# Last quarters of the last two down matrices, read from a copy in eight groups of rows

## The reference, cut to what matters

```python
# hierarchical_moe, 32 experts, top 2 for each of the 256 tokens, for layer l = 0 and 1
hid = jax.nn.silu(xb @ w_gate[e]) * (xb @ w_up[e])      # w_gate, w_up: 1024 x 512 per expert
y = (hid @ w_down[e]) * g_b[:, None]                    # w_down: 512 x 1024 per expert
x = x + (sum of y over each token's experts)
# behind layer 0: a recurrent mixer (lru); behind layer 1: the second block (gated feed-forward, mixers)
```

## Time and profile before

| | us |
|---|---|
| median of the three runs shown | 2074.73 |
| lowest, highest | 2074.47, 2076.21 |
| span of the profiled execution, first to last instruction | 2072.5 |
| tail of layer 0: SP's first quarter to the end of the wait for the last | 500.6 to 532.1 |
| tail of layer 1, the same | 1019.4 to 1053.0 |

### The profile page before, as it was taken

How to read it: one execution, slowest core, us unless ns; L and a number is a source line. 1 busy time by engine, 2 the same in 40 slices (tenths; PEclk the granted TensorE clock), 3 DMA queues, 4 the chain that set the end, 5 groups by cost and what they waited for, 6 DMA issues and landing times.

```text
span 2072.5 us, 31532 instructions
## 1 busy us (share of the span) xinstructions
PE 1855.8 (90%) x13948; PEld 1441.8 (70%) x13948; DVE 1014.3 (49%) x1434; ACT 703.5 (34%) x1049; POOL 39.2 (2%) x46
## 2 busy tenths in 40 slices
PE   9987777677998876777799999999999999999999
PEld 7944333343795433343478889998888888999888
DVE  5722110111672110111158777877777667787666
ACT  6310000000561000000055555655546445465553
POOL 0000000000000000000000003000000000300000
PEclk9999998888999988899899999999999999999999
DMA  9899999999989999999985554545555556445552
GB/s 396 335 418 430 430 431 429 430 430 426 397 333 415 429 431 429 430 430 431 425 327 194 192 207 174 182 170 185 184 204 193 190 183 216 174 160 183 187 195 86
DMA packets 64942, 626.59 MB, mean 302 GB/s; under 512 B 7200, under 2 KB 7328, under 8 KB 14496
## 3 DMA queue, kind: packets, MB, share of 16 engines
q1 hardware_dynamic: 64800, 624.50, 75.4%
HBM read 623.42 MB, written 1.05 MB: 301 GB/s over the span
## 4 chain that ended last, share of the span: by engine, by line
PE 73%; DMA 19%; DVE 4%; ACT 2%; SPq 2%; issue 1%; DVEq 0%; ACTq 0%
PE ps L606 14%; PE ps L609 7%; PE ps L869 7%; DMA dense_ring<-in_moe_w_down 7%; PE ps L550 6%; PE ps L551 6%; PE ps L552 6%; DMA expert_ring_a<-in_moe_w_down 5%; PE ps L860 5%; PE ps L1093 4%; PE ps L1072 4%; DMA work<-in_moe_w_down 4%; PE ps L885 3%; PE ps L849 3%; PE ps L1077 2%; PE ps L1097 2%
## 5 line engine op out<-in xcount | busy, mean ns | idle before, releaser
L1674 DVE TENSOR_TENSOR w_lo<-dense_ring,w_hi 128x1024 fp32r<-128x1024 f32 x398 | 468.9, 1221 | 54.7 <-ACT w_hi L1246 53.7
L1246 ACT CAST w_hi<-dense_ring 128x1024 fp32r<-128x1024 f32 x398 | 397.1, 1048 | 47.1 <-PE ps L552 26.1
L606 PE MATMUL ps<-h_both,w_hi 128*128 128x512 f32 x1344 | 337.4, 393 | 0.8 <-DVE work L2153 0.8
L606 PEld LDWEIGHTS ps<-h_both,w_hi 128*128 128x128 f32 x1344 | 241.8, 189 | 45.5 <-DVE work L2153 2.2
L2020 DVE TENSOR_TENSOR work<-work,ps 128x256 f32<-128x256 f32 x32 | 13.5, 421 | 478.6 <-ACT work L1438 478.6
L609 PEld LDWEIGHTS ps<-h_both,w_lo 128*128 128x128 f32 x1344 | 183.3, 190 | 13.1
L550 PE MATMUL ps<-h_both,w_hi 128*128 128x256 f32 x656 | 188.5, 287 | 0.4 <-DVE h_both L1680 0.3
L609 PE MATMUL ps<-h_both,w_lo 128*128 128x256 f32 x1344 | 187.4, 282 | 0.0
L552 PE MATMUL ps<-h_both,w_lo 128*128 128x256 f32 x656 | 185.6, 283 | 0.0
L551 PE MATMUL ps<-h_both,w_hi 128*128 128x256 f32 x656 | 185.6, 283 | 0.0
L1438 ACT ACTIVATE work<-ps 128x256 f32<-128x256 f32 x32 | 12.3, 383 | 479.8 <-PE ps L860 479.8
(11 more groups left out here) (319 smaller groups left out, 2863.5 us busy)
## 6 DMA issues: line engine op xcount, KB each, us to landing
dense_ring<-in_dense SPq DMA_DIRECT2D x207, 1024.0 KB, 4.9
expert_ring_b<-in_moe_w_up SPq DMA_DIRECT2D x20, 2048.0 KB, 39.8
expert_ring_a<-in_moe_w_gate SPq DMA_DIRECT2D x19, 2048.0 KB, 42.7
expert_ring_a<-in_moe_w_up SPq DMA_DIRECT2D x19, 2048.0 KB, 41.5
dense_ring<-in_moe_w_gate SPq DMA_DIRECT2D x17, 2048.0 KB, 39.9
dense_ring<-in_moe_w_down SPq DMA_DIRECT2D x16, 2048.0 KB, 34.8
expert_ring_b<-in_moe_w_down SPq DMA_DIRECT2D x14, 2048.0 KB, 44.6
dense_ring<-in_moe_w_up SPq DMA_DIRECT2D x14, 2048.0 KB, 39.2
```

What stands on the lines that cost most here:

```text
L606: mm(bank[b + f], w[0][:, f, k, :], h_pairs[:, k, :], start=k == 0, stop=False)
L1246: S.copy(half_of(key, f, 0), tile_of(slot(key), key, f)).then_inc(rounded.up(key, f), 1)
L1674: V.tensor_tensor(half_of(key, f, 1), tile_of(slot(key), key, f), half_of(key, f, 0).bitcast(F32), ALU.subtract).then_inc(remainder.up(key ...
```

## The change

`lay_out` makes a second copy, `last_down`, of the last quarters (columns 3072 to 4096 of the 4096) of the down matrices of experts 30 and 31 of both layers. Its 128 rows are stored in another order: row 8 i + b of the copy is row 16 b + i of the matrix. `piece` reads quarter 3 of the last two matrices from it, through an access pattern whose outermost dimension is eight groups b, then sixteen rows i, then 1024 elements. The destination is the same 128 partitions, and gets the same values. Four DMAs of 512 KB are concerned, the last two of each layer's tail; the other 14 quarters of a tail are loaded as before. Nothing changes on the other engines.

```diff
+LAST_BY_HALF = 2
...
             c = slice(i * EXP_F // parts, (i + 1) * EXP_F // parts)
+            source = matrix_source(l, pr, s)[:, c]
+            if n >= N_MATRIX - LAST_BY_HALF and i == 3:
+                source = a["last_down"][LAST_BY_HALF * l + n - N_MATRIX + LAST_BY_HALF].rearrange("(i b) n -> b i n", b=P // 16)
             said = said_by.up(l) if said_by else event.up(l, pr, s, *(() if i == (parts - 1 if last is None else last) else (i,)))
-            sync.dma_start(dst[:, c], matrix_source(l, pr, s)[:, c]).then_inc(said, 16)
+            sync.dma_start(dst[:, c], source).then_inc(said, 16)
...
         arrays[n] = v.reshape(2 * N_EXP, P, EXP_F)
+    last = arrays["moe_w_down"].reshape(2, N_EXP, P, EXP_F)[:, N_EXP - LAST_BY_HALF:, :, 3 * EXP_F // 4:]
+    arrays["last_down"] = last.reshape(2 * LAST_BY_HALF, P // 16, 16, EXP_F // 4).swapaxes(1, 2).reshape(-1, P, EXP_F // 4)
```

## The result

| | before | after |
|---|---|---|
| median, us | 2074.6 (2073.55 to 2076.21, four runs) | 2092.32 (2089.02 to 2093.91, four runs) |
| ratio | | 1.0086, 95% interval 1.0074 to 1.0098 |
| span of the profiled execution, us | 2072.5 | 2090.2 |

The change costs 17.7 us, 0.86%. The forecast was 2073.4 us in a range of 2072.7 to 2080.0: wrong in sign and far outside the range.

What follows compares the result with a forecast made beforehand. The prediction took each expert layer's last weight transfer as the bound. An earlier landing would save PE 0.69 us a layer, 2 x 0.69 = 1.4 us, so 2074.73 - 1.4 = 2073.4 us, range 2072.7 to 2080.0.

Steps and rivals of the forecast that it cites:

- What bounds the kernel: At each expert layer's end, the chain of waits runs through the very last weight transfer, landing at 532.13 and 1052.96.
- Eight engines carry the two transfers: Last two transfers of each layer: one engine per group, 2.44 us each instead of 1.22 us on sixteen engines.
- write freely: Forecast case, chance 0.35: the eight engines are ahead and write the two transfers unhindered, giving 2073.4 us.
- the slow half is rid of its share: At each layer's end, the eight late engines lose 2 x 1.22 = 2.44 us of work and end earlier.
- 529.7: Forecast end in layer 0 of the slow engines, 532.13 - 2.44; quarter 3 would land near 529.8.
- 534.6: Layer 0 landing of quarter 3 if late engines carry the transfers (chance 0.28), or if shared partitions limit them (chance 0.24).
- the place written is the limit: Rival at quarter 3's landing: the way into the partitions limits transfers; 0 to + 4.9 us, most likely 2077.1; chance 0.24.
- SP, HBM, the dense loads at nothing: Issue of the transfers by SP, their source reads in HBM and earlier dense chunks were each taken to change nothing.
- Which eight engines: Step named most likely to fail: the pattern picks engines that are ahead; the rival of late ones, 2079.6 us, chance 0.28.
- those ahead: About eight DMA engines at each layer's end, some 4.8 us ahead in layer 0 and 4.5 us in layer 1.
- the late half: The other eight DMA engines at each layer's end, whose slowest sets quarter 3's landing at 532.13 in layer 0.

Runs made afterwards that it cites:

- with nothing beside: Changed kernel, its two eight-group transfers issued after the other matrices' quarter 3 landed, dense loads held until these two landed: 2096.81 us.
- the control: Changed kernel with the copy in natural order, 128 rows outermost, the two transfers waiting for ordinary pieces and dense loads waiting for them: 2083.35 us.
- the run with more filler: Changed kernel with 28 filler products instead of 6 on PE between the combine of quarter 1 and the products of quarter 3: 2090.27 us.
- the mixture: Changed kernel with only the last matrix's quarter 3 in eight groups, the one before ordinary, both isolated from other weight and dense loads: 2089.37 us.
- sixteen groups: Changed kernel with the copy read as sixteen groups of eight rows instead of eight of sixteen: 2086.84 us, ratio 1.0056.

## Why the prediction was wrong

**What bounds the kernel, and where the change acts: right.** The chain went through the last transfer before and does so after, and the whole of the 17.7 us arises between that transfer and the next stage, 9.2 and 8.5 us.

**Eight engines carry the two transfers: right.** 32 small packets less; a share of 0.52 when they ran with nothing beside.

**What they cost an engine: the step that failed.** "Each group goes to one engine, so that eight engines carry it, 2.44 us each" took over the rate of an ordinary transfer, 430 / 16 = 27 GB/s an engine, and the forecast had them "write freely". With nothing beside, the engines ran at 254 / 16 = 16 GB/s, a packet of 4 KB in some 256 ns instead of 159. The time from the last issue to the landing was 10.56 us, in the control 5.12: + 5.4 us for the two instead of the + 2.44 that doubling the bytes of an engine gives.

**The untouched pieces: the second half of that step.** I moved work between engines as if they were independent ("the slow half is rid of its share"). In the changed kernel the ordinary pieces slowed down too, to 205 to 239 GB/s over share in all, quarter 2 came 2.7 us late, and the landing was at 539.64 instead of my 529.7 or, at worst, 534.6.

**The rival "the place written is the limit": right in mechanism, too small in size, and given too little.** It had quarter 2's delay, and the idle time before quarter 3 beyond 0.69 us, but 3.1 us at most where 5.50 was measured, and + 4.9 us for the kernel where it was + 17.7. Its bound let one engine of the group and one late engine meet. It left out that the group's own engines meet each other; the Trainium skill's map that I cited was enough to work that out, step by step through a group's rows. I even wrote that a group's four ports are shared with another group of sixteen, and drew no price from it. "Against it" I had put that something other than writes delays eight engines; that says nothing on what two writers do to each other.

**No term for PE's clock.** Idle from 534.3, it was at 1.2 GHz when the data came: + 1.69 and + 1.45 us, shown by the run with more filler.

**SP, HBM, the dense loads at nothing: right.** SP issued the last piece at 516.35, and the copy alone cost nothing.

**"Which eight engines" was the wrong worry.** I named it the likeliest step to fail. By the packets, six of the eight are among those ahead, as the forecast took it, and two are late. The rate fell once the first of them had started, so the forecast would have been wrong with all eight ahead as well; that last is argued, not run.

Open is how three parties share. In the changed kernel an ordinary engine meets the group's pair only where that pair stands. By the Trainium skill's map (SBUF — State Buffer, section "Door 1: The DMA port swizzle") the groups' four pairs stand on four of the sixteen ports at a time; an ordinary engine of the late half would then be alone for three quarters of the time, and I estimate from that and from 27 GB/s a port 8 x (0.75 x 27 + 0.25 x 9) + 8 x 11 = 268 GB/s for all sixteen, with 11 GB/s as a middle between a port shared by two and by three. Measured are 205 to 239 over share, and of the 316 packets of 4 KB that start between 526 and 534 none took under 220 ns, so no ordinary engine was free for three quarters of the time. The order of size is right, the rest isn't explained: a queue that backs up at a shared port would do it, which no run here shows.

No run beat the kernel before. PE could use 0.69 us a layer of an earlier landing; 1.4 us is under what can be measured, so I tried no version for it.

## What to carry to other kernels

Before you spread a transfer otherwise than by 128 rows, write down for each engine which partitions it writes at each step, and see whether two meet at one way in: with nothing beside, the rate over share was 254 to 286 GB/s where by the map they meet in pairs and 350 to 367 where they don't. (The one exception is the mixture.) A transfer that makes its engines meet also slows the ordinary transfers beside it, so price it by the whole stream (little over half the rate while it is in flight: 205 to 239 for 410), not by its own bytes. And read GB/s over DMA share: a share of 1 can be sixteen slow engines. Where the trace has each packet's time, that is clearer still.

## What was not expected of the hardware

- 2 MB in such transfers, 0.3% of the kernel's 626.59 MB, cost 0.86% of its time.
- Two plain transfers of 64 partitions side by side cost as much as sixteen groups: 2086.52 and 2086.84 us.
- A transfer in eight groups that touches only half of the partitions still pulled all engines down to 238 GB/s at a share of 1.05.
- One transfer in eight groups, behind an ordinary one and with nothing else beside, ran at its engines' ordinary 159 ns a packet; two in a row took 256.
- PE had been idle for some 5.5 us when its next products ran at half the clock, and they took 3.62 us for 1.93.
